# A seventh weight unit loaded ahead of the expert stage, with three rounded buffers in place of four until it is used

## The chip, the cores and the metric

The program runs on 1 core of one Trainium2 chip. The metric is device time in microseconds (us). Three runs of the kernel before gave 1814.45, 1812.17 and 1812.78 us, a median of 1812.78.

## What is computed

The reference is three layers over 256 tokens of width 1024 in float32. The first is a mixer layer (sparse attention beside a state space model) with a feed-forward part, the second a short convolution with a feed-forward part, the third a mixer of two attentions followed by a mixture of experts. The change touches the mixture of experts alone:

```python
h  = rms_norm(x, ffn_norm)
g_w, g_idx   = top_k(softmax(h @ w_group + b_group), 1)      # one of 8 groups per token
top_v, top_i = top_k(e_sel, 2)                                # two of its 8 experts
gate = g_w * softmax(top_v)
out  = sum over the two experts e of gate[e] * ((silu(h @ w1[e]) * (h @ w3[e])) @ w2[e])
x    = x + out
```

`w1` and `w3` are 1024x512 and `w2` is 512x1024, 64 experts each: 192 matrices of 2 MB, all of which are read from HBM once.

## The kernel before

**Units.** Each of the 192 expert matrices is one unit: a tile of 128 partitions by 4096 words. A group of experts has 24 units, in the order of the list `MOE` (lines 661 to 664): w1 and w3 of experts 0, 1 and 2, then w2 of expert 0, w1 and w3 of expert 3, w2 of expert 1 and so on, so that units 6, 9, 12 and 15 are w2 products. There are 8 groups, 192 units; `m_unit` counts the units that TensorE has finished.

**Stages of a unit.** SyncE loads it into one of six slots of `ring` (`expert_load`, line 794). ScalarE writes the rounded copy, here called the high copy, into one of four buffers `w_hi` (`first_hi` at line 1742 for units 0 to 3, ahead of the stage, and `split_hi` at line 1974 for the rest). VectorE subtracts it from the raw weights and leaves the low copy in the slot itself (`split_lo`, line 2566). TensorE multiplies with both: 16 matmuls in `expert_in` (line 1510) or `expert_out` (line 1541). The high copy of a unit may be written when its buffer's last unit is finished, and a slot is loaded again when its unit is finished:

```python
sp.wait_ge(m_unit, n * NM + (u - SLOTS + 1))        # line 810: load of unit u waits for unit u - 6
act.wait_ge(m_unit, n * NM + (u - HI_SLOTS + 1))    # line 1973: high copy of unit u waits for unit u - 4
```

**Order on each engine.** All of it is written out by hand, and each engine works its list in order.

- ScalarE, behind unit u: it copies the product out (`hidden_raw`, line 1987), for some u it computes the silu (line 1992), the rounded half of the hidden layer (`hidden_hi`, line 1996) or copies the turned selection (line 1982), and then it writes the high copy of unit u + 4.
- VectorE, at position u: it writes the low copy of unit u + 3, then for some u `hidden` (line 2699, the product of silu and the other half) and `hidden_lo` (line 2704), and at u = 8 the selection of the next group (line 2637). `hidden` of expert e stands behind the low copies of units 5, 7, 9 and 12 for e = 0, 1, 2 and 3, and `hidden_lo` behind those of units 6, 8, 10 and 13.
- `hidden_hi` of expert e on ScalarE waits for `hidden` of that expert on VectorE. It stands at u = 3, 5, 7 and 10 for the first four experts.
- TensorE: unit u, then at u = 2, 4, 6 and 9 the `fold` of experts 0 to 3 (line 1524, 16 small matmuls), which needs both products of that expert copied out, and `hidden` of the expert before.

**Ahead of the stage.** The six slots are filled as the last units of the layer before leave them (lines 796 to 799), and the sixth load waits for `out2_11`, the last product of the output projection. ScalarE writes high copies 0, 1 and 2 before the projection is finished. The fourth buffer of `w_hi` lies where the high half of the projection's second weight unit lies, so high copy 3 is written once `out2_11` is ready (`first_hi(3)`, line 1960). VectorE writes low copies 0 and 1. Then come the norm, the router and the gathering of the tokens of group 0, and TensorE begins unit 0. `passes` (how often all groups are gone through) is 1 with these inputs.

The kernel's functions:

Of the kernel before, what the change touches and what calls it, by code (L numbers as in the profile page):

```python
# [254 lines left out]
def program(nc, d, out):  # L255
    with ExitStack() as ctx:
# [146 lines left out]
        w_hi = [first_w_hi, second_w_hi, carve(SLOT, of=arena_r), last_hi]  # L403
# [266 lines left out]
        MOE_SLOT = [(W.next + u) % SLOTS for u in range(len(MOE))]  # L670
        MOE_BEFORE = [W.last[s] for s in MOE_SLOT[:SLOTS]]
        MOE_BASE = [W.dmas[s] * 16 for s in MOE_SLOT]
        PER_SLOT = len(MOE) // SLOTS
        NM = len(MOE)

# [46 lines left out]
        def _(sp):  # L722
# [73 lines left out]
            for u, (kind, e) in enumerate(PREFETCH):  # L796
                if MOE_BEFORE[u]:
                    sp.wait_ge(*MOE_BEFORE[u])
                expert_load(kind, e, u)
# [18 lines left out]

            with sp.Fori(0, passes) as p:
                with sp.Fori(0, N_GROUPS - 1) as g:  # L820
                    n = sp.snap(p * N_GROUPS + g)
                    rest_of_group(n, g * PER_GROUP)
                    first_of_group(n, g * PER_GROUP + PER_GROUP)
                n = sp.snap(p * N_GROUPS + (N_GROUPS - 1))
                rest_of_group(n, N_EXPERTS - PER_GROUP)
                with sp.If(p + 1 < passes):
                    first_of_group(n, 0)
            sp.wait_ge(out_ready, 2)
# [9 lines left out]
        def _(pe):  # L838
# [596 lines left out]
            def occupy(n):  # L1435

                for _ in range(n):
                    mm(bank("idle"), w_hi[0][:, 0:P], w_hi[0][:, P:P + 512], start=True, stop=True)
# [61 lines left out]
            def expert_in(u, n):  # L1500
# [6 lines left out]
                u_hi, u_lo = w_hi[u % HI_SLOTS], ring_r[MOE_SLOT[u]]  # L1507
# [20 lines left out]
            def expert_out(u, n, p=None):  # L1528
# [10 lines left out]
                u_hi, u_lo = w_hi[u % HI_SLOTS], ring_r[MOE_SLOT[u]]  # L1539
# [75 lines left out]
            occupy(3)  # L1615
            with pe.Fori(0, passes) as p:
                with pe.Fori(0, N_GROUPS - 1) as g:
                    n = pe.snap(p * N_GROUPS + g)
                    pe.wait_ge(m_xg_lo, n + 1)
                    for u, (kind, e) in enumerate(MOE):  # L1620
                        if kind == "w2":
                            expert_out(u, n)
                        else:
                            expert_in(u, n)
                        if u == 0:
                            with pe.If(g < 1):
                                pe.wait_ge(r_gate, 2)
                                gates_of(n)
                        if u in FOLD_AT:
                            fold(FOLD_AT[u], n)  # L1630
                        if u == SEND_AT:
                            with pe.If(g > 0):
                                send_back(n)
                        if u == SELT_AT:
                            turn_selection(n)
                        if u == GATHER_AT:
                            pe.wait_ge(m_selT, n + 1)
                            gather(n + 1)
                            gates_of(n + 1)
# [20 lines left out]
                with pe.If(p + 1 < passes):  # L1660
                    pe.wait_ge(m_scd, n * 4 + 6)
                    gather(n + 1)


        @block.scalar
        def _(act):
# [72 lines left out]
            def first_hi(u):  # L1739

                act.wait_ge(landed[MOE_SLOT[u]], MOE_BASE[u] + 16)
                A(w_hi[u], ring[:, MOE_SLOT[u], :], ACT.Copy).then_inc(m_hi, 1)
# [217 lines left out]
            first_hi(3)  # L1960
# [7 lines left out]
            def split_hi(u, n):  # L1968

                at = u % NM  # L1970

                act.wait_ge(landed[MOE_SLOT[at]], n * (16 * PER_SLOT) + (MOE_BASE[at] + 16 * (u // SLOTS + 1)))
                act.wait_ge(m_unit, n * NM + (u - HI_SLOTS + 1))
                A(w_hi[u % HI_SLOTS], ring[:, MOE_SLOT[at], :], ACT.Copy).then_inc(m_hi, 1)  # L1974
# [36 lines left out]

            with act.Fori(0, passes) as p:
                with act.Fori(0, N_GROUPS - 1) as g:
                    n = act.snap(p * N_GROUPS + g)
                    for u in range(NM):
                        results(u, n)
                        if u == GATHERED_AT:
                            gathered(n + 1)
                        if u < NM - 1:
                            split_hi(u + HI_SLOTS, n)  # L2020
                    act.wait_ge(m_unit, n * NM + NM)
                    for i in range(2):
                        result_hi(i)
                    split_hi(NM - 1 + HI_SLOTS, n)
# [23 lines left out]
                with act.If(p + 1 < passes):  # L2048
                    for u in range(NM, NM + HI_SLOTS):
                        split_hi(u, n)  # L2050
                    gathered(n + 1)
            n = act.snap(passes * (4 * N_GROUPS))
# [10 lines left out]
        def _(dve):  # L2063
# [498 lines left out]
            def split_lo(u, n):  # L2562

                dve.wait_ge(m_hi, n * NM + (u + 1))
                raw = ring[:, MOE_SLOT[u % NM], :]
                V.tensor_tensor(ring_r[MOE_SLOT[u % NM]][:, :], raw, w_hi[u % HI_SLOTS].bitcast(F32), ALU.subtract).then_inc(m_lo, 1)  # L2566

            split_lo(0, 0)
            split_lo(1, 0)
# [112 lines left out]
            split_lo(2, 0)  # L2682
# [28 lines left out]

            with dve.Fori(0, passes) as p:
                n = dve.snap(p * N_GROUPS)
                with dve.If(p > 0):
                    dve.wait_ge(m_sc, n * 4 + 4)
                    for i, (tc, h) in enumerate(RES):
# [278 lines left out]
```

## Time and profile before

| | |
|---|---|
| median of 3 runs | 1812.78 us (1812.17 to 1814.45) |
| the profiled execution | 1814.1 us |
| its span, first to last instruction | 1812.3 us |
| granted TensorE clock over the span | 0.994 |
| TensorE busy | 1733.4 us, 96% |
| VectorE busy | 1575.9 us, 87% |
| ScalarE busy | 1219.2 us, 67% |
| GpSimd busy | 125.3 us, 7% |
| loads of expert weights | 192 of 2048 KB |

The span is 1.8 us shorter than the profiled execution's own time, which is 1.3 us above the median. Times in a timeline are counted from the first instruction. A row of a timeline has the start and the length in us, the engine, the line of the kernel, what is written and read with its shape, how many instructions are merged in it, and in square brackets how long the engine had been idle and what ended that. A length runs to the time at which the result is written; the next instruction of the engine starts some 0.1 us before that.

### The profile page before, as it was taken

What the parts mean: (1) busy time and instruction counts of PE and PEld (TensorE: products, weight loads), DVE (VectorE), ACT (ScalarE), POOL (GpSimd) and SP (SyncE); (2) the same over time, 40 slices, a digit from 0 to 9 for tenths busy, and PEclk for the clock granted to TensorE, in tenths of its full rate; (3) what the DMA queues carried; (4) which work ended last, traced back from release to release, by engine and by line L of the source; (5) the groups of instructions that cost most, each with busy time, mean ns of one, the idle gap of its engine ahead of it and who ended that gap; (6) DMA issues with size and microseconds to landing.
All of it is one profiled execution on the core that took longest, in us unless ns stands there. A gap on an engine that the chain in (4) does not pass through costs nothing.

```text
span 1812.3 us, 25062 instructions
## 1 busy us (share of the span) xinstructions
PE 1733.4 (96%) x9708; PEld 1478.8 (82%) x9708; DVE 1575.9 (87%) x1383; ACT 1219.2 (67%) x955; POOL 125.3 (7%) x142
## 2 busy tenths in 40 slices
PE   8999999999999999989999999989999999999998
PEld 7977888889888889978877877778777777787776
DVE  6777777789577786587999999999999999999997
ACT  5555454443334355446788989889898898888886
POOL 1255000000000010441000000000000000000000
PEclk9999999999999999999999999999999999999999
DMA  7521345553354555226799999999999999999995
GB/s 288 193 93 71 140 178 202 208 239 148 121 192 177 203 200 217 96 118 244 309 427 428 428 429 428 429 429 428 429 428 428 430 427 428 428 428 429 428 426 241
DMA packets 41389, 544.25 MB, mean 300 GB/s; under 512 B 4720, under 2 KB 4848, under 8 KB 6640
## 3 DMA queue, kind: packets, MB, share of 16 engines
q1 hardware_dynamic: 41328, 543.39, 72.8%
q8 instruction: 43, 0.70, 0.2%
q14 instruction: 18, 0.15, 0.0%
HBM read 542.33 MB, written 1.05 MB: 300 GB/s over the span
## 4 chain that ended last, share of the span: by engine, by line
PE 60%; DMA 13%; issue 7%; ACT 6%; DVE 5%; POOL 0%; DVEq 0%; ACTq 0%; SPq 0%
PE psum L1510 16%; DMA ring<-in_w 13%; PE psum L1053 9%; PE psum L1070 7%; PE psum L893 6%; PE psum L1055 4%; PE psum L1524 4%; ACT arena_r L1974 4%; PE psum L1541 3%; DVE ring_r L2566 2%; PE psum L936 2%; PE psum L1273 1%; PE psum L953 1%; PE psum L1448 1%; PE psum L1416 1%
## 5 line engine op out<-in xcount | busy, mean ns | idle before, releaser
L2566 DVE TENSOR_TENSOR ring_r<-ring,arena_r 128x4096 fp32r<-128x4096 f32 x191 | 842.4, 4418 | 16.0 <-ACT arena_r L1974 12.6
L1974 ACT ACTIVATE arena_r<-ring 128x4096 fp32r<-128x4096 f32 x188 | 682.5, 3630 | 63.7 <-DMA ring<-in_w 62.8
L1510 PE MATMUL psum<-arena_r,stream_r 128*128 128x512 f32 x1024 | 409.2, 400 | 10.5 <-DVE stream_r L2656 7.9
L1510 PE MATMUL psum<-ring_r,stream_r 128*128 128x512 f32 x1024 | 401.1, 392 | 0.0
L1053 PE MATMUL psum<-stream_r,arena_r 128*128 128x512 f32 x704 | 250.6, 398 | 2.1 <-DVE stream_r L2111 1.7
L1510 PEld LDWEIGHTS psum<-arena_r,stream_r 128*128 128x128 f32 x1024 | 193.6, 189 | 55.3 <-DVE ring_r L2566 9.6
L1758 ACT ACTIVATE arena_r<-ring 128x3072 fp32r<-128x3072 f32 x40 | 111.0, 2776 | 181.2 <-DMA ring<-in_ffn 181.2
L1510 PEld LDWEIGHTS psum<-ring_r,stream_r 128*128 128x128 f32 x1024 | 193.5, 189 | 39.0 <-issue 0.5
L1055 PE MATMUL psum<-stream_r,ring_r 128*128 128x256 f32 x704 | 197.6, 281 | 0.0
L1541 PE MATMUL psum<-arena_r 128*128 128x512 f32 x512 | 162.9, 399 | 11.6 <-DVE arena_r L2704 10.6
L1053 PEld LDWEIGHTS psum<-stream_r,arena_r 128*128 128x128 f32 x704 | 132.2, 188 | 35.1 <-issue 3.1
L1541 PE MATMUL psum<-ring_r,arena_r 128*128 128x512 f32 x512 | 159.5, 392 | 0.0
L893 PE MATMUL psum<-stream_r,ring_r 128*128 128x256 f32 x776 | 142.7, 284 | 0.0
L1055 PEld LDWEIGHTS psum<-stream_r,ring_r 128*128 128x128 f32 x704 | 133.0, 189 | 1.5
L2256 DVE TENSOR_TENSOR ring_r<-ring,arena_r 128x3072 fp32r<-128x3072 f32 x40 | 134.1, 3351 | 0.0
L1541 PEld LDWEIGHTS psum<-arena_r 128*128 128x128 f32 x512 | 94.3, 189 | 37.5 <-DVE arena_r L2704 13.5
L893 PEld LDWEIGHTS psum<-stream_r,ring_r 128*128 128x128 f32 x776 | 114.9, 192 | 0.9 <-issue 0.8
L1541 PEld LDWEIGHTS psum<-ring_r,arena_r 128*128 128x128 f32 x512 | 96.7, 189 | 21.0
L1070 PE MATMUL psum<-arena_r 128*128 128x512 f32 x352 | 101.4, 391 | 0.0
L1524 PEld LDWEIGHTS psum<-small,arena 128*128 128x128 f32 x512 | 63.8, 191 | 43.3 <-ACT arena L1987 31.0
L893 PE MATMUL psum<-stream_r,arena_r 128*128 128x256 f32 x416 | 94.0, 283 | 0.3 <-DVE ring_r L2086 0.3
L1524 PE MATMUL psum<-small,arena 128*128 128x64 f32 x512 | 67.5, 275 | 26.6 <-ACT arena L1987 26.5
(354 smaller groups left out, 2438.6 us busy)
## 6 DMA issues: line engine op xcount, KB each, us to landing
ring<-in_w SPq DMA_DIRECT2D x192, 2048.0 KB, 13.0
ring<-in_ffn SPq DMA_DIRECT2D x44, 1536.0 KB, 6.3
ring<-in_w_in SPq DMA_DIRECT2D x8, 2048.0 KB, 7.9
ring<-in_out_w SPq DMA_DIRECT2D x7, 2048.0 KB, 7.9
ring<-in_in_w SPq DMA_DIRECT2D x6, 2048.0 KB, 10.9
ring<-in_l_in SPq DMA_DIRECT2D x8, 1536.0 KB, 9.1
ring<-in_proj SPq DMA_DIRECT2D x2, 2048.0 KB, 8.6
ring<-in_in_w SPq DMA_DIRECT2D x2, 1024.0 KB, 9.8
```

The lines of the kernel that those rows point to most:

```text
L893: last = mm(dst, w[:, at:at + width], a[:, k, :], start=(k == 0 and i == 0), stop=(k == KD - 1 and i == 2))
L936: last = mm(bank(name)[:, 0:width], a[:, k, tc * P:(tc + 1) * P], w[:, k * n:k * n + width], start=(k == 0 and i == 0), stop=(k == KD - 1 ...
L1053: mm(gu[b % 2][m], u_hi[:, at:at + P], both_halves[:, :, k, :], start=(k == 0), stop=(k == KD - 1), skip_group_check=True)
L1055: return mm(gu[b % 2][m][:, 1, :], u_lo[:, at:at + P], xnT_r[:, k, :], start=False, stop=(k == KD - 1), skip_group_check=True)
L1070: last = mm(bank(f"ffn{n}_{tc}{h}"), a[:, b % 2, tc * P:(tc + 1) * P], w[:, 2048 + h * 512:2560 + h * 512], start=(start and i == 0), stop ...
L1510: last = mm(dst, xg[:, k, :], b[:, k * D_EXPERT:(k + 1) * D_EXPERT], start=(k == 0 and b is u_hi), stop=(k == KD - 1 and b is u_lo))
L1524: last = mm(psum[:, T_BANK, (i * NE + j) * CAP:(i * NE + j + 1) * CAP], h_raw[:, e % 2, i, j * P:(j + 1) * P], turn, start=True, stop=True)
L1541: return mm(psum[:, Y_BANK[h], :], hT[:, e % 3, j, :], b[:, j * D + h * 512:j * D + (h + 1) * 512], start=(e == 0 and j == 0 and b is u_hi ...
L1758: A(arena_r[:, FFN_HIGH[n][nxt % FFN_RING]:][:, 0:FFN_WORDS], ring[:, slot, 0:FFN_WORDS], ACT.Copy).then_inc(w_high, 1)
L1974: A(w_hi[u % HI_SLOTS], ring[:, MOE_SLOT[at], :], ACT.Copy).then_inc(m_hi, 1)
L2256: V.tensor_tensor(ring_r[slot][:, 0:FFN_WORDS], ring[:, slot, 0:FFN_WORDS], arena_r[:, FFN_HIGH[n][nxt % FFN_RING]:][:, 0:FFN_WORDS].bitca ...
L2566: V.tensor_tensor(ring_r[MOE_SLOT[u % NM]][:, :], raw, w_hi[u % HI_SLOTS].bitcast(F32), ALU.subtract).then_inc(m_lo, 1)
```

## The change

- The seventh unit (unit 6) is loaded ahead of the stage as well. It goes into the words of the arena that held the projection's high half, which were the fourth rounded buffer, `last_hi`. The load stands right behind the sixth load in SyncE's list and waits for `out2_11`. Its low copy is left in the same place.
- With that, units 0 to 8 of the first group use three rounded buffers in turn; from unit 9 on there are four again. `first_hi(3)` ahead of the stage is gone. ScalarE writes high copy u + 3 behind unit u for u = 0 to 6, behind unit 6 also high copy 10, and high copy u + 4 from there on.
- In the first group, loads 7 to 12 wait for units 0 to 5, the slot that they go into; from load 13 on, load u waits for unit u - 6 as before. The slots of all later units are one further round the ring.
- The first group of the first pass is written out ahead of the loops on every engine, and the loop over groups starts at 1. For a second pass, the first group is written out again inside the `If` at the end of the pass.

```diff
-        w_hi = [first_w_hi, second_w_hi, carve(SLOT, of=arena_r), last_hi]
+        w_hi = [carve(SLOT, of=arena_r), last_hi, first_w_hi, second_w_hi]
+        seventh, seventh_lo = arena[:, D:D + SLOT], last_hi
...
+        AHEAD = SLOTS + 1
...
+        def high_of(u, early):
+            if early and u < 3 * 3:
+                return w_hi[(2, 3, 0)[u % 3]]
+            return w_hi[u % HI_SLOTS]
...
@@ SyncE
-            for u, (kind, e) in enumerate(PREFETCH):
+            for u in range(SLOTS):
                 if MOE_BEFORE[u]:
                     sp.wait_ge(*MOE_BEFORE[u])
-                expert_load(kind, e, u)
+                first_load(u)
+            sp.wait_ge(*O.ready("out2_11"))
+            first_load(SLOTS)
             sp.wait_ge(x_rows, NT)
...
+            for u in range(AHEAD, NM):
+                sp.wait_ge(m_unit, u - AHEAD + 1 if u <= AHEAD + SLOTS - 1 else u - SLOTS + 1)
+                first_load(u)
+            first_of_group(0, PER_GROUP)
             with sp.Fori(0, passes) as p:
-                with sp.Fori(0, N_GROUPS - 1) as g:
+                with sp.Fori(1, N_GROUPS - 1) as g:
...
@@ TensorE
+            group_of_units(0, True, True)
             with pe.Fori(0, passes) as p:
-                with pe.Fori(0, N_GROUPS - 1) as g:
+                with pe.Fori(1, N_GROUPS - 1) as g:
...
                 with pe.If(p + 1 < passes):
                     pe.wait_ge(m_scd, n * 4 + 6)
                     gather(n + 1)
+                    n = pe.snap(n + 1)
+                    group_of_units(n, True)
...
@@ ScalarE
             square_row(5, 1)
-            first_hi(3)
...
+            def split_hi(u, n, early=False):
+                at_work = HI_SLOTS - 1 if early and u <= 3 * 3 else HI_SLOTS
+                act.wait_ge(*unit_landed(u, n, early))
+                act.wait_ge(m_unit, n * NM + (u - at_work + 1))
+                A(high_of(u, early), raw_of(u, early), ACT.Copy).then_inc(m_hi, 1)
...
+            def group_of_units(n, early=False):
+                for u in range(NM):
+                    results(u, n)
+                    if u == GATHERED_AT:
+                        gathered(n + 1)
+                    if early and u <= SLOTS:
+                        split_hi(u + 3, n, True)
+                    if u < NM - 1 and not (early and u < SLOTS):
+                        split_hi(u + HI_SLOTS, n, early)
...
+            group_of_units(0, True)
...
@@ VectorE
+            def group_of_units(n, following, opening, early=False):
+                if opening:
+                    gates_in_fold(n)
+                for u in range(NM):
+                    split_lo(u + 3, n, early and u + 3 < NM)
+                    if u in FOLD_AT:
+                        hidden(FOLD_AT[u], n)
+                    if u in TURN_AT:
+                        hidden_lo(TURN_AT[u], n)
...
+            group_of_units(0, 1, True, True)
```

## Rows read from the trace of the kernel before

**Rows 1.** The page: busy time, share of the span and instructions of each engine.
```profile
PE 1733.4 (96%) x9708; PEld 1478.8 (82%) x9708; DVE 1575.9 (87%) x1383; ACT 1219.2 (67%) x955; POOL 125.3 (7%) x142
```

**Rows 2.** Stretches: length, busy time per engine, TensorE clock, DMA share, GB/s.
```profile
866.00:878.00 12.00, 10.94 (x65) 9.12 (x64) 9.49 (x30) 3.56 (x4) 0.00 (x0) 1.00 0.14 39
880.00:960.00 80.00, 75.91 (x383) 62.47 (x382) 79.65 (x32) 69.85 (x45) 0.00 (x0) 1.00 1.00 424
...
1000.00:1790.00 790.00, 748.14 (x3772) 620.15 (x3770) 776.76 (x336) 695.28 (x418) 0.00 (x0) 1.00 1.01 428
```

**Rows 3.** Loads of units 6, 13, 16 and 29: issue, and time to landing.
```profile
L794 SPq DMA_DIRECT2D ring<-in_w x1: 342/342/342, 876.1 to 876.1; - x1
...
DMA to landing us min/median/max: 8.5/8.5/8.5
...
L794 SPq DMA_DIRECT2D ring<-in_w x1: 333/333/333, 908.0 to 908.0; - x1
...
DMA to landing us min/median/max: 11.4/11.4/11.4
...
L794 SPq DMA_DIRECT2D ring<-in_w x1: 333/333/333, 921.7 to 921.7; - x1
...
DMA to landing us min/median/max: 13.1/13.1/13.1
...
L794 SPq DMA_DIRECT2D ring<-in_w x1: 333/333/333, 988.5 to 988.5; - x1
...
DMA to landing us min/median/max: 10.0/10.0/10.0
```

**Rows 4.** Timeline of ScalarE behind units 0, 2, 3 and 5.
```profile
876.42 3.63 ACT L1974 ACTIVATE arena_r<-ring 128x4096 fp32r<-128x4096 f32 x1
...
886.25 3.63 ACT L1974 ACTIVATE arena_r<-ring 128x4096 fp32r<-128x4096 f32 x1
...
892.69 0.42 ACT L1996 ACTIVATE arena_r<-arena 128x256 fp32r<-128x256 f32 x1 [2.33 <-DVE arena L2699]
...
893.28 3.63 ACT L1974 ACTIVATE arena_r<-ring 128x4096 fp32r<-128x4096 f32 x1
...
902.35 3.62 ACT L1974 ACTIVATE arena_r<-ring 128x4096 fp32r<-128x4096 f32 x1
```

**Rows 5.** Timeline of VectorE: low copies 3 to 8 and one hidden step.
```profile
879.23 13.09 DVE L2566 TENSOR_TENSOR ring_r<-ring,arena_r 128x4096 fp32r<-128x4096 f32 x3
892.24 0.42 DVE L2699 TENSOR_TENSOR arena<-psum,arena 128x256 f32<-128x256 f32 x1
892.57 4.42 DVE L2566 TENSOR_TENSOR ring_r<-ring,arena_r 128x4096 fp32r<-128x4096 f32 x1
...
897.24 4.42 DVE L2566 TENSOR_TENSOR ring_r<-ring,arena_r 128x4096 fp32r<-128x4096 f32 x1
...
901.91 4.41 DVE L2566 TENSOR_TENSOR ring_r<-ring,arena_r 128x4096 fp32r<-128x4096 f32 x1
```

**Rows 6.** Chain that ended last, TensorE: a fold, units 7 and 8, fold 3.
```profile
883.64 1.73 PE psum L1524 x16
...
904.11 7.35 PE psum L1510 x32
```
```profile
915.83 1.10 PE L1524 MATMUL psum<-small,arena 128*128 128x64 f32 x8 [0.73 <-ACT arena L1987]
```

**Rows 7.** VectorE's low copies 957 to 984; unit 23; a stretch behind it.
```profile
L2566 DVE TENSOR_TENSOR ring_r<-ring,arena_r 128x4096 fp32r<-128x4096 f32 x7 | 31.0, 4424 | 1.6 <-ACT arena_r L1974 1.3
```
```profile
982.94 0.50 PE L1541 MATMUL psum<-arena_r 128*128 128x512 f32 x1 [1.79 <-DVE arena_r L2704]
```
```profile
980.00:985.00 5.00, 3.21 (x12) 2.27 (x11) 5.00 (x3) 4.22 (x3) 0.00 (x0) 0.87 1.02 436
```

**Rows 8.** The page: DMA queue of instructions. Timeline of ScalarE at the end.
```profile
q8 instruction: 43, 0.70, 0.2%
```
```profile
1803.55 0.60 ACT L2055 ACTIVATE xn<-psum 128x512 f32<-128x512 f32 x1 [0.41 <-PE psum L1604]
```

## Prediction before the result

> **What bounds the kernel now.** I began with the page. TensorE is busy for 96% of the span [rows 1], which suggests a kernel bound by TensorE, but that share is a mean over stages. So I cut the span into stretches. From 880 us on, the DMA engines are busy for the whole of every stretch at 424 to 428 GB/s [rows 2]: the expert stage is a stream of weights. A unit of 2048 KB takes 2.097 MB / 428 GB/s = 4.9 us. The stage ends when the last unit has landed and has been worked. Anything that moves the landings moves the end by as much, and nothing else does.
>
> The stretch ahead of it is the opening that the change aims at: between 866 and 878 us the DMA engines have a share of 0.14 [rows 2]. Six units have landed, and the load of unit 6 waits for unit 0 and is issued at 876.1 [rows 3]. One more load in that hole would put every later landing 4.9 us earlier, if the queue never runs dry afterwards.
>
> The same table shows why that "if" matters. From 880 to 960 us VectorE is busy for 79.65 of 80 us, against 776.76 of 790 (98.3%) later [rows 2]. So two things are saturated at once in the first 80 us. Whoever makes VectorE late there makes TensorE late, then the loads that wait for TensorE, then perhaps the stream.
>
> How much lateness does the stream bear? A load issued into an empty queue lands 8.5 us later. Load 13 lands 11.4 us after its issue, load 16 after 13.1, load 29 after 10.0 [rows 3]. What is above 8.5 is time that the load spent queued behind others, and so its reserve: 2.9 us for load 13, 4.6 for load 16, 1.5 for load 29.
>
> **The DMA side of the change.** Loads 6 to 12 land 4.9 us earlier, load 7 being issued at 876.1, where load 6 was, and so on. Load 13, however, still waits for unit 7, the same unit as before, while the queue ahead of it is 4.9 us shorter. Its reserve of 2.9 becomes -2.0. So even with no delay in the computation the gain is at most 2.9 us, not 4.9, and each further microsecond by which unit 7 is late costs one. The seventh load itself costs nothing: it waits for the same product as the sixth, so nothing on SyncE's list is held up, and the row of norm weights behind it is wanted only at the end. The DMA engines are idle then [rows 2]; without that hole it would cost its 4.9 us.
>
> **The compute side.** High copy 3 is no longer written ahead, and ScalarE is one unit less ahead of VectorE until unit 9. I follow VectorE copy by copy. Before, low copies 3, 4 and 5 run back to back from 879.23, 13.09 us for three, hence 4.34 apart [rows 5].
>
> 1. High copy 3 takes the place that high copy 4 had behind unit 0: 876.42 plus 3.63 is 880.05 [rows 4]. Low copy 3 starts at 880.1 instead of 879.2: **0.9 us late**.
> 2. High copy 5 takes the place of high copy 6: 886.25 plus 3.63 is 889.9 [rows 4]. Low copy 5 starts there instead of at 879.23 + 2 x 4.34 = 887.9: **2.0 late**.
> 3. Here is the step that costs. Behind low copy 5 VectorE does `hidden` (892.24) [rows 5], ScalarE waits for it (2.33 us idle), rounds it at 892.69, and starts the next high copy at 893.28 [rows 4]. That is 5.4 us after low copy 5 started. Before, the copy in that place was number 7, needed two low copies later, so its 3.63 us were hidden. Now it is number 6, the very next that VectorE wants. So VectorE waits for ScalarE, which has just waited for VectorE: 889.9 + 5.4 + 3.63 = 898.9 instead of 892.57 [rows 5], **6.4 late**.
> 4. Low copy 7 follows at once, high copy 7 being finished by then (898.9 + some 0.7 + 3.6 = 903.2, against 898.9 + 4.7 = 903.6): still 6.4 late.
> 5. The same loop again through `hidden` of expert 1. Before, 902.35 - 897.24 = 5.1 us from low copy 7 to the high copy [rows 4, 5]; now 903.6 + 5.1 + 3.6 = 912.4 instead of 901.91: **10.5 late**.
> 6. Behind unit 6 ScalarE writes two high copies and has its old lead back. VectorE, which had only 0.35 us idle in 80 [rows 2], keeps the 10.5.
>
> **From there to the stream.** Unit 7 has the fold of expert 2 in front, and that fold needs `hidden` of expert 1, which stands behind low copy 7: 903.6 + 4.3 + 0.4 = 908.4. Add 1.75 for the fold, 3.9 for the unit (half of 7.35 and the end of the last matmul) [rows 6] and 0.2 to the issue: load 13 is issued at 914.3 and lands 8.5 later, at 922.8. Before, it landed at 908.0 + 11.4 = 919.4. Load 12, one unit's 4.9 us ahead of that and now 4.9 us earlier, has landed at 909.6, so the engines run dry for several us, which the old kernel never does here.
>
> Load 16 waits for unit 10, and unit 10 stands behind fold 3, which waits for ScalarE [rows 6] and by way of the high copy before that for `hidden` of expert 2, behind low copy 9. So its issue is 10.5 late: 921.7 + 10.5 + 8.5 = 940.7. Before, it landed at 921.7 + 13.1 = 934.8. The stream is now **5.9 us behind** the old one. The landings between (14 and 15) come no later by this count.
>
> Afterwards VectorE catches up in its idle time, but a landing lost is not won back. One more place is tight: load 29, reserve 1.5 [rows 3], waits for unit 23, and unit 23 for `hidden_lo` behind low copy 24 [rows 7]. VectorE's idle time up to there is 0.35 to 960 [rows 2] and 1.6 after it [rows 7], so it is still 10.5 - 1.9 = 8.6 late against a stream that is 5.9 late: another 8.6 - 5.9 - 1.5 = 1.2. TensorE's granted clock is 0.87 in the stretch around that unit, so part of it at 1.2 GHz and the rest at 2.4 GHz, after an idle time of 1.79 us [rows 7]. I assume the same fall again in the same place; without it unit 23 ends 1.6 us sooner and the 1.2 is gone.
>
> **Sum.** 5.9 + 1.2 = 7.1 us. The tail behind the last landing is not touched. The rest of the edit goes at nothing: a branch per group is removed, and the straight first group is the same instructions in the same order. Against the profiled execution that is 1814.1 + 7.1 = 1821.2; the difference carried to the median is 1812.78 + 7.1 = **1819.9 us**.
>
> Bounds of what the trace does not show. Issue to landing into an empty queue is 8.5 us in the one row that has it [rows 3] and cannot be above the 10.0 of load 29, which had others ahead of it; it could be 0.2 less or more elsewhere, and I take 8.5. Entering the loop at group 1 instead of 0 costs between 0 and the 0.3 us by which the engines' issue times scatter. Idle times of TensorE of 3 to 4 us, new in this stage, may lower its clock in units 6 and 8; priced by the fall in unit 23 that is up to 1.6 us each, but both stand in front of VectorE's wait and not behind it, so I take 0 and keep 1.6 for the range.
>
> On the landing time the rows and a rule part. The Trainium skill, DMA: Bandwidth & Descriptors (Anatomy of one DMA), gives about 2.0 us plus the bytes over 436 GB/s, which for a unit is an estimate of 6.8 us; by it every landing of the starved queue would come 1.7 us sooner and the sum would be 5.4. It is written for the path through GpSimd, and the row of this kernel's own load says 8.5.
>
> **The rivals.**
> - *The waits are absorbed (not slower).* Place: unit 7, on which load 13 waits. If VectorE's loss stayed at the 2.0 us of step 2, load 13 would land at 908.0 + 2.0 + 8.5 = 918.5, 0.9 us earlier than before: 1811.9. With no loss at all 2.9 are won: 1809.9. It decides the case if unit 7 is less than 2.9 us late. For it: the exchange of step 3 is argued from order, not seen. Against it: the 2.33 us in which ScalarE waits for `hidden` [rows 4] show the loop half closed already. Chance 0.10.
> - *Only one loop bites.* If high copy 8 were ready by some reserve I missed, VectorE stays 6.4 late and load 16 lands at 921.7 + 6.4 + 8.5 = 936.6, 1.8 us late: 1814.6. Chance 0.10.
> - *Instruction fetch.* The `If` at the end of the pass now holds a whole group, which one pass jumps over. Fetches of instructions take 0.2% of 16 engines' 1812 us for 43 packets, 1.35 us each [rows 8]; ScalarE stands 0.41 us idle there [rows 8], so 0.9 us would come through: 1820.8, and 1821.7 with as much at the loop's entry. Chance 0.10. The Trainium skill, Runtime: NRT & Kernel Launch (Instruction fetch mechanics), has it that a taken branch to a page outside the two held ones stalls for a fetch; no row shows such a stall.
> - *The clock falls on the path.* 1.6 us more: 1821.5. Chance 0.10.
> - *The seventh unit does not come early.* Its load could only be late by standing behind the sixth. Even then, from load 13 on the time is set by the units, so the sum is the same.
>
> **How the numbers follow.** The forecast has 0.60, with 1817.8 to 1820.8 as its own range. 0.2% of the time is 3.6 us, about what a measurement of this kernel can tell from no change. The first two rivals lie within it, and I leave 0.03 for a gain of more: the reserve of load 13 forbids it. Same 0.17. Slower 0.80. The range goes from 1814.3, just under the second rival, to 1822.8, the clock and the fetch together; it leaves out the first rival and a little above.
>
> **What would show it.** Right: ScalarE's first high copy behind unit 0 is number 3; two idle times of VectorE of 4 to 4.5 us at about 894.5 and 908.3, ended by ScalarE's high copy; low copy 8 at 912.4; a hole in the DMA row around 909 to 918 and load 13 issued at 914; the seventh unit landed by 872. Wrong: a DMA share of 1.00 through 905 to 925, or low copy 8 before 905.

## The result, and the profile after

| | before | after |
|---|---|---|
| median | 1812.68 us of 4 runs | 1823.59 us of 4 runs (1822.76 to 1824.36) |
| the profiled execution | 1814.1 | 1824.4 |
| its span | 1812.3 | 1822.5 |

The ratio is 1.0060, with a 95% interval of 1.0045 to 1.0075: 10.9 us slower. The direction is as forecast, and the time is 3.7 us above the forecast and 0.8 us above the range.

The page of the kernel after, and the three stretches of [rows 2] in it, the first two 0.86 us earlier because unit 0 begins that much earlier here (columns as in [rows 2]):

```profile
PE 1737.9 (95%) x9708; PEld 1480.8 (81%) x9708; DVE 1574.8 (86%) x1383; ACT 1200.6 (66%) x942; POOL 125.0 (7%) x142
...
q8 instruction: 49, 0.80, 0.2%
```
```profile
865.14:877.14 12.00, 11.03 (x66) 9.17 (x65) 9.49 (x30) 2.28 (x3) 0.00 (x0) 1.00 0.49 187
879.14:959.14 80.00, 71.11 (x341) 57.88 (x340) 70.60 (x28) 65.70 (x41) 0.00 (x0) 0.96 0.88 360
1000.00:1790.00 790.00, 750.15 (x3767) 622.30 (x3766) 775.27 (x338) 678.43 (x407) 0.00 (x0) 0.99 1.01 428
```

The change does what it says: the hole in the transfers ahead of the stage is partly filled, a share of 0.49 in place of 0.14 [rows 2]. But in the 80 us behind it VectorE is busy for 70.60 us instead of 79.65, and the DMA engines, which were never idle there, have a share of 0.88. At 360 GB/s in place of 424 [rows 2] they move 5.1 MB less, which is 2.4 units or 12 us of the stream. Less the 4.9 us of the unit that was loaded early, some 7 us are lost there by this estimate. From 1000 us on the stream runs at its old rate again.

Where VectorE and ScalarE lost it, in their timelines (copies 3 and 4, 5, `hidden`, copies 6, 7 and 8 on VectorE; then high copy 3, `hidden_hi` of expert 0, high copy 6, `hidden_hi` of expert 1 and high copy 8 on ScalarE):

```profile
879.21 8.76 DVE L2621 TENSOR_TENSOR ring_r<-ring,arena_r 128x4096 fp32r<-128x4096 f32 x2 [0.67 <-ACT arena_r L2021]
889.04 4.42 DVE L2621 TENSOR_TENSOR ring_r<-ring,arena_r 128x4096 fp32r<-128x4096 f32 x1 [1.07 <-ACT arena_r L2021]
893.38 0.42 DVE L2754 TENSOR_TENSOR arena<-psum,arena 128x256 f32<-128x256 f32 x1
898.06 4.42 DVE L2621 TENSOR_TENSOR arena_r<-arena,arena_r 128x4096 fp32r<-128x4096 f32 x1 [4.26 <-ACT arena_r L2021]
...
902.74 4.42 DVE L2621 TENSOR_TENSOR ring_r<-ring,arena_r 128x4096 fp32r<-128x4096 f32 x1
...
911.49 4.43 DVE L2621 TENSOR_TENSOR ring_r<-ring,arena_r 128x4096 fp32r<-128x4096 f32 x1 [3.99 <-ACT arena_r L2021]
```
```profile
875.56 3.62 ACT L2021 ACTIVATE arena_r<-ring 128x4096 fp32r<-128x4096 f32 x1
...
893.84 0.42 ACT L2043 ACTIVATE arena_r<-arena 128x256 fp32r<-128x256 f32 x1 [4.35 <-DVE arena L2754]
894.42 3.61 ACT L2021 ACTIVATE arena_r<-arena 128x4096 fp32r<-128x4096 f32 x1
...
907.53 0.42 ACT L2043 ACTIVATE arena_r<-arena 128x256 fp32r<-128x256 f32 x1 [4.74 <-DVE arena L2754]
907.85 3.61 ACT L2021 ACTIVATE arena_r<-ring 128x4096 fp32r<-128x4096 f32 x1
```

The two engines wait for each other in turn. `hidden` ends at 893.80, ScalarE has waited 4.35 us for it, then writes high copy 6, and VectorE has waited 4.26 us for that. The same again behind copy 7, with 4.74 and 3.99. Low copy 8 starts at 911.49, where it started at 901.91 [rows 5]: 9.6 us late, and 10.4 if counted from unit 0.

The loads that answer to [rows 3] (units 13, 14, 15, 16, 27 and the last one, 191), and after them the loads of 27 and 191 in the kernel before:

```profile
L830 SPq DMA_DIRECT2D ring<-in_w x1: 328/328/328, 913.4 to 913.4; - x1
...
DMA to landing us min/median/max: 7.4/7.4/7.4
...
L830 SPq DMA_DIRECT2D ring<-in_w x1: 327/327/327, 921.5 to 921.5; - x1
...
DMA to landing us min/median/max: 7.3/7.3/7.3
...
L830 SPq DMA_DIRECT2D ring<-in_w x1: 328/328/328, 925.1 to 925.1; - x1
...
DMA to landing us min/median/max: 9.7/9.7/9.7
...
L830 SPq DMA_DIRECT2D ring<-in_w x1: 327/327/327, 931.2 to 931.2; - x1
...
DMA to landing us min/median/max: 8.6/8.6/8.6
...
L825 SPq DMA_DIRECT2D ring<-in_w x1: 327/327/327, 985.9 to 985.9; - x1
...
DMA to landing us min/median/max: 9.5/9.5/9.5
...
L825 SPq DMA_DIRECT2D ring<-in_w x1: 327/327/327, 1784.3 to 1784.3; - x1
...
DMA to landing us min/median/max: 17.0/17.0/17.0
```
```profile
L794 SPq DMA_DIRECT2D ring<-in_w x1: 332/332/332, 977.6 to 977.6; - x1
...
DMA to landing us min/median/max: 11.2/11.2/11.2
...
L794 SPq DMA_DIRECT2D ring<-in_w x1: 328/328/328, 1775.8 to 1775.8; - x1
...
DMA to landing us min/median/max: 15.8/15.8/15.8
```

Landings are issue plus landing time. Load 13 lands at 920.8 against 919.4, load 14 at 928.8 against 925.0 and load 15 at 934.8 against 929.9; load 16 at 939.8 against 934.8, 5.0 late (5.8 counted from unit 0); load 27 at 995.4 against 988.8, 6.6 late; load 191 at 1801.3 against 1791.6, 9.7 late. So 3.1 us were lost behind unit 27, and not by loads that were issued too late: they were lost at loads 30 and 191, which were issued 11.6 and 17.0 us ahead of their landings. The first place is in ScalarE's timeline, high copies 29 and 30:

```profile
1005.21 3.64 ACT L2021 ACTIVATE arena_r<-ring 128x4096 fp32r<-128x4096 f32 x1 [0.73 <-DMA ring<-in_w]
...
1011.64 3.64 ACT L2021 ACTIVATE arena_r<-ring 128x4096 fp32r<-128x4096 f32 x1 [0.58 <-DMA ring<-in_w]
```

Both copies start as their unit lands, 6.43 us apart where the stream brings one in 4.9, although load 30 was issued 11.6 us ahead. A smaller part is behind the last unit, on SyncE: the first two of the three output stores, after, and then the second one before.

```profile
1817.29 0.34 SPq L873 DMA_DIRECT2D out<-x  x1
1817.95 1.26 SPq L875 DMA_DIRECT2D out<-x  x1
```
```profile
1808.54 0.34 SPq L831 DMA_DIRECT2D out<-x  x1
```

The middle store takes 0.9 us more to issue. Writing out the first group and giving it another order are thus two suspects, and the runs take them apart.

### The profile page after: what moved, and what is told of

The parts are those of the page before. It is cut to its first block, busy times and chain, and to the rows that moved or that the text cites. A ratio compares the mean times of both kernels' runs of the same rounds, so it can differ in the third digit from the quotient of the medians.

```text
span 1822.5 us, 24836 instructions
## 1 busy us (share of the span) xinstructions
PE 1737.9 (95%) x9708; PEld 1480.8 (81%) x9708; DVE 1574.8 (86%) x1383; ACT 1200.6 (66%) x942; POOL 125.0 (7%) x142
## 4 chain that ended last, share of the span: by engine, by line
PE 51%; DVE 11%; issue 11%; DMA 11%; ACT 6%; POOL 0%; DVEq 0%; ACTq 0%; SPq 0%
DMA ring<-in_w 10%; PE psum L1554 10%; PE psum L1097 8%; DVE ring_r L2621 7%; PE psum L1114 6%; PE psum L937 6%; PE psum L1099 4%; ACT arena_r L2021 4%; PE psum L1568 3%; PE psum L1585 2%; PE psum L980 2%; PE psum L1317 1%; PE psum L997 1%; PE psum L1492 1%; PE psum L1460 1%
## 5 line engine op out<-in xcount | busy, mean ns | idle before, releaser
L1585 PE MATMUL psum<-arena_r 128*128 128x512 f32 x520 | 163.7, 397 | 13.1 <-DVE arena_r L2759 10.4
## 6 DMA issues: line engine op xcount, KB each, us to landing
ring<-in_in_w SPq DMA_DIRECT2D x6, 2048.0 KB, 10.4
```

The lines of the kernel that those rows point to most:

```text
L1585: return mm(psum[:, Y_BANK[h], :], hT[:, e % 3, j, :], b[:, j * D + h * 512:j * D + (h + 1) * 512], start=(e == 0 and j == 0 and b is u_hi ...
```

## The experiments

Ratios are to the kernel before on the same chip, with the 95% interval; medians are of 10 or 11 runs unless another count stands. "Over before" is the median less that of the kernel before in the same series (1813.19, 1813.54, 1813.09 and 1813.12 us in the four series), 10.9 us for the changed kernel. In the first expectations theory A is that of the prediction (order, then stream), and theory B that the written-out group costs something by itself; the later expectations each say what theory A is there.

**Writing the group out and nothing else.** The buffers, order and loads of before, but group 0 ahead of the loops on every engine:

```diff
-        w_hi = [carve(SLOT, of=arena_r), last_hi, first_w_hi, second_w_hi]
+        w_hi = [first_w_hi, second_w_hi, carve(SLOT, of=arena_r), last_hi]
...
-            sp.wait_ge(*O.ready("out2_11"))
-            first_load(SLOTS)
...
+            first_hi(3)
...
-                    if early and u <= SLOTS:
-                        split_hi(u + 3, n, True)
```

> The first group written out ahead of the loops and nothing else: six units loaded ahead, four rounded buffers, high copy 3 written ahead, as in the kernel before. Theory A (the loss comes from VectorE and ScalarE waiting for each other, and what comes after load 16 follows from the queue of loads having run short): no difference, 1812.7 within 1.5 us, every landing within 1 us of before. Theory B (writing the group out costs by itself, through more fetches of instructions on the DMA engines and a long jump at the end): 3 to 5 us slower, the landings slipping where instructions are fetched.

1815.77 us, ratio 1.0013 (1.0004 to 1.0022), 2.6 us over before. So this part of the edit is not free, though 2.6 us is less than the 3 to 5 of theory B.

**The seventh load not early.** The changed kernel, with unit 6 loaded behind unit 0 as before:

```diff
-            sp.wait_ge(*O.ready("out2_11"))
-            first_load(SLOTS)
...
+            sp.wait_ge(m_unit, 1)
+            first_load(SLOTS)
             for u in range(AHEAD, NM):
```

> As the changed kernel, but the load of unit 6 waits for unit 0 instead of the last product of the projection, so nothing is loaded in the hole. Theory A: from load 13 on each load is issued when its unit is finished and the queue is dry, so the 4.9 us lead was already lost there: load 13 still lands at about 920.8, the total within 1.5 us of the changed kernel's 1823.6. Rival (the early load is worth something that the rest hides): 4.9 us slower than the changed kernel, 1828.5.

1822.52 us of 4 runs, ratio 1.0050 (1.0035 to 1.0065), 9.3 us over before; with the load early 1.0060 (1.0045 to 1.0075) and 10.9. The intervals overlap, and load 13 lands at 920.0 here: the load that the change is about wins nothing that shows, and nearly the whole loss stands without it.

**The order on VectorE.** `hidden` of experts 0 and 1 moves ahead of the low copy at its place, so that ScalarE need not wait for that copy:

```diff
                 for u in range(NM):
+                    sooner = early and u in (2, 4)
+                    if sooner:
+                        hidden(FOLD_AT[u], n)
                     split_lo(u + 3, n, early and u + 3 < NM)
-                    if u in FOLD_AT:
+                    if u in FOLD_AT and not sooner:
                         hidden(FOLD_AT[u], n)
```

> As the changed kernel, but in the first group VectorE does the hidden step of experts 0 and 1 ahead of low copies 5 and 7 instead of behind them, so that ScalarE does not wait for it before high copies 6 and 8. Theory A: both waits of VectorE of 3.8 to 4.5 us go, low copy 8 starts 2 to 3 us later than before instead of 10.5, load 13 lands about 2 us earlier than in the kernel before, and the total is 1810 to 1813. Theory B: the same less 3 to 5 us that remain, 1814 to 1817. Rival (the third buffer itself is what is short, not the order): VectorE still waits for high copies 6 and 8, total 1820 or more.

1815.70 us, ratio 1.0011 (1.0002 to 1.0020), 2.5 us over before: two operations of 0.42 us that change places with a low copy take 8.4 of the 10.9 us back. Its VectorE timeline, low copies 5 and 6, and the stretch:

```profile
890.36 4.43 DVE L2621 TENSOR_TENSOR ring_r<-ring,arena_r 128x4096 fp32r<-128x4096 f32 x1 [0.73 <-ACT arena_r L2021]
894.93 4.43 DVE L2621 TENSOR_TENSOR arena_r<-arena,arena_r 128x4096 fp32r<-128x4096 f32 x1
```
```profile
880.00:960.00 80.00, 75.13 (x373) 61.48 (x371) 78.30 (x31) 72.35 (x45) 0.00 (x0) 1.00 0.96 400
```

The idle time of 4.26 us is gone, VectorE is busy for 78.30 us of 80, and the DMA share is 0.96. This is the loop of the prediction's step 3, opened at one end. The total is where theory B had it (1814 to 1817).

**The order on ScalarE.** The other end: high copies 6 and 8 ahead of the `hidden_hi` that waits.

```diff
+                    swapped = early and u in (3, 5)
+                    if swapped:
+                        hidden_raw(u, n)
+                        split_hi(u + 3, n, True)
+                        hidden_hi(TURN_AT[u], n)
...
```

> As the changed kernel, but ScalarE writes high copies 6 and 8 ahead of the rounded halves of hidden 0 and 1, which is the other way to break the same loop. Theory A: low copy 8 about 2.5 us later than in the kernel before, load 13 lands about 0.7 us earlier than there, total 1811 to 1814. If the order did not matter: 1823.

1819.38 us of 6 runs, ratio 1.0029 (1.0017 to 1.0041), 6.2 us over before: 4.7 us are back, a miss against what was expected. VectorE still waits for high copies 7 and 8:

```profile
901.66 4.42 DVE L2629 TENSOR_TENSOR ring_r<-ring,arena_r 128x4096 fp32r<-128x4096 f32 x1 [1.79 <-ACT arena_r L2021]
...
906.85 4.43 DVE L2629 TENSOR_TENSOR ring_r<-ring,arena_r 128x4096 fp32r<-128x4096 f32 x1 [0.43 <-ACT arena_r L2021]
```

Low copy 8 starts at 906.85, between the 911.49 of the changed kernel and the 901.91 of before [rows 5]. What runs ahead on ScalarE here is a copy of 3.63 us, and what it passes is later by as much; on VectorE it was an operation of 0.42 us. That this is why the form wins less is read from these rows alone, and no run tests it.

**What in the written-out group costs.** First, without the group inside the `If` at the end of the pass (a second pass is left out; so it is in the other kernels below that have a short or no `If` or a loop from 1 or 2 on one engine alone, and with one pass the work timed is complete), on SyncE, TensorE, ScalarE and VectorE:

```diff
                 with sp.If(p + 1 < passes):
                     first_of_group(n, 0)
-                    rest_of_group(n + 1, 0)
-                    first_of_group(n + 1, PER_GROUP)
...
-                    n = pe.snap(n + 1)
-                    group_of_units(n, True)
```

> As e1, but the first group of a second pass, which is never executed with these inputs, is left out of the If at the end of the pass, so that the jump at the end is as short as in the kernel before; a second pass would be computed wrongly. Theory A (the jump makes SyncE fetch instructions between its last stores): the gap from the second to the third output store goes back from 1.8 us to some 0.4 us, and the total falls by about 1 us against e1, to 1814.5. Rival (the stall belongs to the place of the code, not to the jump): no change, 1815.5.

1815.53 us, ratio 1.0011 (1.0002 to 1.0020), 2.0 us over before. The middle store is issued in 0.34 us again; with the long `If` in the same kernel it took 1.75:

```profile
1810.20 0.34 SPq L857 DMA_DIRECT2D out<-x  x1
```
```profile
1806.92 1.75 SPq L859 DMA_DIRECT2D out<-x  x1
```

The cause of the stall at the stores is thus shown: it comes and goes with what the `If` holds. In the changed kernel a packet of the instruction queue, q8, travels during that store, and with the short `If` none does. But 2 us remain. Next, group 1 written out too (loops from 2), to double them if they are per group:

```diff
             group_of_units(0, True, True)
+            group_of_units(1, False)
...
-                with pe.Fori(1, N_GROUPS - 1) as g:
+                with pe.Fori(2, N_GROUPS - 1) as g:
```

> As e5, with the second group written out ahead of the loops too, which doubles what the first one adds: TensorE fetches another group's code, five to six pages, while the stream runs. Theory A (each fetched page can hold one DMA engine up, and a hitch of up to 1.5 us in the landings stays): one or two hitches more than e5 in the stretch from 1110 to 1230 us, total 0 to 3 us above e5, most likely 1.5. Rival (the cost of writing the group out has nothing to do with fetches): equal to e5 within 0.5 us, no new hitches.

1815.97 us, ratio 1.0012 (1.0003 to 1.0021), 2.4 us over before. That is 0.4 us more than with one group, where theory A had most likely 1.5 and its rival less than 0.5. The intervals are too wide to tell twice the cost from the same. The rows side with theory A: in the profiled execution loads 30, 72 and 190 land 6.1, 6.2 and 5.7 us behind the one before, each with a packet of instructions in that gap, and from the landing of load 17 to that of load 191 it takes 855.8 us, against 853.3 with one group and 851.9 before. Its total is low all the same (1815.2), because load 17 had landed 3.0 us earlier than in the run with one group.

**Combinations.** By the diffs above: the VectorE order with the load not early, then the VectorE order with the short `If`.

> As e3 (hidden first), but the load of unit 6 waits for unit 0. Now the computation is only 2.8 us late, so the lead of the early load should not be wholly lost. Theory A: by the reserve of load 13 in the kernel before (2.9 us), the stream without the early load is just not starved by 2.8 us, the landings stay as in e1, total 1814 to 1817, that is within 2 us of e3; the early load is worth at most 2.9 us. Rival (the early load is worth its full 4.9 us once the order is mended): 1820 or more.

1814.84 us, ratio 1.0010 (1.0001 to 1.0020), 1.3 us over before; with the early load it was 2.5. Even with the order mended the early load shows no gain.

> As e3 (hidden first) without the first group of a second pass in the If. Theory A: about 1 us less than e3, 1814.7, still not under the kernel before, because the fetches of the group's code remain. If it comes under 1812 the seventh unit does pay once its order and the jump are mended.

1814.59 us, ratio 1.0006 (0.9997 to 1.0015), 1.1 us over before. This is the best form of the change. It is still not under the kernel before, from which it can't be told apart.

**On which engine.** The first is the short form with TensorE's loop as it was; the second is the kernel before with TensorE's first group alone written out. The diff is that of the first, the second turns it round:

```diff
-            group_of_units(0, True, True)
             with pe.Fori(0, passes) as p:
-                with pe.Fori(1, N_GROUPS - 1) as g:
+                with pe.Fori(0, N_GROUPS - 1) as g:
```

> As e5 (first group written out, no second pass), but TensorE's own list keeps the loop of the kernel before, so that it does not fetch the group's code a second time. If TensorE's fetches cause the 2 us that writing the group out costs: 1813.5 within 1 us, 43 packets in the queue of instructions as before, and no hitch of over 1 us in the landings between 990 and 1240 us. If it is the other engines' lists: 1815.5 as e5.

> The kernel before with TensorE's first group alone written out ahead of its loop. If TensorE's fetches are the cause: 1815.5 as e5, one hitch of 1.0 to 1.5 us near a fetch between 990 and 1110 us. If not: 1813.5 as the kernel before.

1812.53 us, ratio 1.0000 (0.9991 to 1.0009), and 1814.67 us, ratio 1.0010 (1.0001 to 1.0019): 0.6 us under before and 1.6 over. The two intervals just overlap, so the rows have to bear it out that the cost is TensorE's. The DMA view of both for 1092 to 1101 us (packets, MB, share of 16 engines), and ScalarE's high copies there, all but the one at 1095.08 started by their landing; first TensorE alone:

```profile
q8 instruction: 1, 0.02, 0.8%
```
```profile
1094.22 3.63 ACT L1977 ACTIVATE arena_r<-ring 128x4096 fp32r<-128x4096 f32 x1 [0.86 <-DMA ring<-in_w]
...
1100.67 3.63 ACT L1977 ACTIVATE arena_r<-ring 128x4096 fp32r<-128x4096 f32 x1 [2.34 <-DMA ring<-in_w]
```

Then all but TensorE:

```profile
q1 hardware_dynamic: 265, 3.85, 100.5%
```
```profile
1095.08 3.62 ACT L1999 ACTIVATE arena_r<-ring 128x4096 fp32r<-128x4096 f32 x1
...
1099.82 3.64 ACT L1999 ACTIVATE arena_r<-ring 128x4096 fp32r<-128x4096 f32 x1 [0.64 <-DMA ring<-in_w]
```

A packet of instructions travels in the full stream, and the copy behind its landing starts 6.45 us after the one before it instead of 4.74. Over the whole run the instruction queue q8 moves 43 packets before and with TensorE's loop kept, 47 with TensorE's group written out (with or without the others), 49 with the group in the `If` as well, and 52 with two groups. Between 990 and 1700 us, in the middle of the stream, it moves none before and with TensorE's loop kept, and 5 with the group written out on TensorE, by the same view:

```profile
q8 instruction: 5, 0.08, 0.0%
```

With all but TensorE written out, another queue (q14) moves three packets of half that size in this stretch, and no landing there is late.

The meeting of packet and late landing can be counted. The 14 profiled executions of this case have 2436 landings from load 18 on, 4.9 us apart as a rule. Of these, 34 come more than 5.2 us behind the one before. Five of them are load 27, whose issue is late in those runs. Of the other 29, 26 have a q8 packet in the gap, while of all 2436 gaps only 177 have one. So where a landing was late without a late issue, a fetch was nearly always there. The reverse does not hold: 122 of the 148 packets delayed no landing by that much.

**One load made later.** In the short form of the written-out group, load 27 waits for one unit more:

```diff
-            first_of_group(0, PER_GROUP)
+            for u, (kind, e) in enumerate(PREFETCH):
+                sp.wait_ge(m_unit, NM - SLOTS + u + 1 + (1 if u == 3 else 0))
+                expert_load(kind, PER_GROUP + e, u)
```

> As e5, but load 27 alone waits for one unit more, so it is issued some 3.7 us later, about 7.5 us ahead of the time at which it used to land (11.2 less 3.7). Theory R1 (a load lands on time if issued 8.5 us ahead, as the prediction took it): it lands some 1 us late, and all behind it too; total 1 us over e5. Theory R2 (a full stream needs some 10 us): it lands 2 to 2.5 us late. No effect on landings before it.

1815.34 us, ratio 1.0012 (1.0003 to 1.0022). That is 2.3 us over before, against 2.0 without the later load. The total doesn't tell the two apart. The rows do. Load 27 in the short form, then with the later issue:

```profile
L811 SPq DMA_DIRECT2D ring<-in_w x1: 328/328/328, 977.7 to 977.7; - x1
...
DMA to landing us min/median/max: 11.2/11.2/11.2
```
```profile
L811 SPq DMA_DIRECT2D ring<-in_w x1: 328/328/328, 980.1 to 980.1; - x1
...
DMA to landing us min/median/max: 9.4/9.4/9.4
```

This execution runs 1.2 us ahead of the other at unit 26, so the load is issued 3.6 us later and lands 1.9 later. It had 1.7 us to give, not the 11.2 - 8.5 = 2.7 of the prediction's rule. But that does not make 9.4 us a floor for every load in the full stream: in the changed kernel load 19 lands 9.1 us after its issue and no later behind load 18 than the stream brings one in (4.90), and in the run with the VectorE order and the load not early load 27 does so with 9.2.

**The changed kernel with the short `If`.**

> The changed kernel with the first group of a second pass left out of the If, as e5 is to e1. If the parts add up: the gap between the last output stores goes, 0.9 us less than the changed kernel's 1823.6, so 1822.7; two waits of VectorE of 3.8 to 4.5 us at about 894 and 907 as in the changed kernel, and load 13 issued when the queue is empty. If the long jump cost more than the one gap: 1821 or less.

1821.96 us of 5 runs, ratio 1.0049 (1.0035 to 1.0063), 8.8 us over before against 10.9. VectorE's two idle times are there as expected, 4.26 us ahead of 898.05 and 3.99 us ahead of 911.47, and the middle store takes 0.34 us. The stall at the stores is 0.9 of the 2.1; the rest is within the intervals.

## Why the prediction was right or wrong

**Right: the compute side.** All six steps happened. High copy 3 is the first behind unit 0; VectorE's idle times are 4.26 and 3.99 us; low copy 8 at 911.5 was forecast for 912.4, with all of the difference in the 0.86 us by which unit 0 began sooner (875.56 against 876.42 [rows 4]). The run with `hidden` ahead shows it as the cause, and its price in the end: 10.9 - 2.5 = 8.4 us.

**Right in the main: the DMA side.** The seventh unit had landed at 869.5. Load 13 was issued at 913.4 (914.3 less the 0.86 is 913.4), and the transfers ran dry ahead of it, as in this stretch (columns as in [rows 2]):

```profile
909.00:914.00 5.00, 4.34 (x22) 3.32 (x21) 2.51 (x1) 5.00 (x3) 0.00 (x0) 1.00 0.00 0
```

Load 16 landed 5.8 us late counted from unit 0, where 5.9 was the sum. The rival by which the seventh unit does not come early gave the same sum, and the run without it is not above the changed kernel. The rivals "the waits are absorbed" and "only one loop bites" are refuted by the second idle time of 3.99 us.

**Luck in how near the 5.9 came.** The step had load 16 set the loss by its own late issue. But load 15 was already 5.8 us late counted from unit 0, and load 16 landed 4.95 us behind it, as the stream brings them in. The loss arose at loads 13, 14 and 15, and two of its terms were off, in opposite directions.

- Landing into an empty queue: loads 13 and 14 landed 7.4 and 7.3 us after their issue, not 8.5 [rows 3]. The Trainium skill, DMA: Bandwidth & Descriptors (Anatomy of one DMA), whose rule for the path through GpSimd gives an estimate of 6.8, was nearer to these two than the row was. Load 16 took 8.6, with load 15 still ahead of it.
- TensorE's clock: the bounds priced a fall in units 6 and 8 at nothing, since both stand in front of VectorE's wait. Unit 8 does not. It starts at 915.97, when low copy 8 is written, after 2.63 us in which TensorE was idle, and more than half of it runs at 1.2 GHz:

```profile
915.97 0.79 PE L1554 MATMUL psum<-arena_r,stream_r 128*128 128x512 f32 x1 [2.63 <-DVE ring_r L2621]
```
```profile
916.00:920.00 4.00, 4.00 (x11) 3.20 (x12) 4.00 (x2) 3.22 (x2) 0.00 (x0) 0.58 0.96 410
```

It ends at 921.32, after 5.35 us in place of 3.7 (half of the 7.35 of [rows 6]), and load 14, which waits for it, was issued at 921.5. Up to 1.6 us of load 14's lateness is thus the clock's. The rival "the clock falls on the path" had that event right, but it did not come on top of the sum. How much of it reached load 16 no run shows.

**Wrong: the size of a load's reserve in the running stream, and the place of the last loss.** The step said that all above 8.5 is reserve, that load 29 is tight and that the clock falls again at unit 23. The clock did not fall there: load 29 is only as late as the stream. It fell earlier, in unit 8 as above and in the stretch below, ahead of which TensorE had been idle for 1.82 us. There its mean was 0.72, so part of the time at 1.2 GHz and the rest at 2.4:

```profile
894.00:900.00 6.00, 6.00 (x28) 5.21 (x29) 1.94 (x1) 6.00 (x6) 0.00 (x0) 0.72 1.01 429
```

This one lies in front of VectorE's wait, as the bounds had it, and low copy 8 came no later than forecast. Load 27 was the tight one instead. It was issued 8.3 us late and landed 6.6 late, so it had 1.7 us to give, as in the run with the later load, and not 2.7. The stream ahead of it was 5.8 late, so it lost 0.8 us. Counted from unit 0 the landings are 5.8 us late at load 16 and 7.5 at load 27 (6.6 + 0.9), where the sum had 7.1. That these are near is partly luck too: of the 1.7 between them load 27 explains 0.8, and 0.7 were lost at load 20, where a packet of instructions lies (next point).

**Wrong, and the reason for the miss: "The rest of the edit goes at nothing: a branch per group is removed, and the straight first group is the same instructions in the same order."** The instructions are the same, but q8 moves more of them: 49 packets in place of 43 [rows 8]. The bound of 0 to 0.3 us covered the entry of the loop alone. The runs price it in two parts. TensorE's written-out group costs 1.6 us alone and 2.0 with the other engines' in the short form, by medians whose intervals reach some 1.6 us to either side. The group in the `If` costs 0.9 us at SyncE's second store, and 1.4 in the kernel whose only edit is the group written out. The instruction-fetch rival, with a chance of 0.10, had the right resource. It had the wrong engine: ScalarE's idle time at the jump is 0.39 us after and was 0.41 [rows 8]. And it missed the larger part, since it asked what the fetching engine waits for and not what a fetch does to the stream. The Trainium skill, Runtime: NRT & Kernel Launch (Instruction fetch mechanics), has a taken branch to a page that is not held stall for a fetch. SyncE's row of 1.26 us against 0.34 agrees with that.

Added up against the profiled executions: -0.9 for the earlier unit 0, 7.5 up to load 27, 2.8 from there to the end of the last unit (which is 9.4 late) and 0.8 at the stores make 10.2, and so do the spans. The 2.8 and the 0.8 are in no term of the prediction's sum.

**Open.** Why one fetched packet delays a landing by some 1.5 us was not tried. Its own time is 0.8% of 16 engines' 9 us, 1.2 us on one of them. One reading is that a unit has landed only when the slowest of its parts has, and that a packet counts only where it meets that part; that would fit the 122 packets of 148 that delayed nothing much. It is an argument and not shown. That fetches cause the late landings at all rests on the kernels with and without TensorE's written-out group and on the count of packets in late gaps; no run fetched without changing the code. Of the 3.1 us between loads 27 and 191, load 30 took 1.5 and load 191 took 1.5, and both have a packet in their gap (1008.4 in 1005.2 to 1011.6, and 1798.0 in 1794.8 to 1801.2). In the kernel before, the packet near the last load starts at 1795.8, 4.2 us after that load has landed. Which packets meet a landing thus shifts with the timing of the kernel. Not tried either is the seventh unit in its best order with TensorE's first group left in its loop.

## What to carry to other kernels

A buffer fewer is a change of order: where two engines hand work to and fro, write down which copy the other engine needs next, because a lead of one unit on either side can be what keeps a wait on each from closing into a loop. A prefetch is worth only what its queue keeps, so ask at once which later load is issued at the old time, and take its reserve from a run in which it is issued later, not from a landing into an empty queue. And a loop unrolled for one group isn't free in a kernel bound by its transfers: leave the engine with the most instructions in its loop, as the run that kept TensorE's loop did, with the time of before (ratio 1.0000).

## What was not expected of the hardware

- Instructions that TensorE's written-out group adds travel with the weights: four packets more on the instruction queue (43 to 47), 1.6 to 2.0 us by the medians, lasting to the end of the kernel. Of 29 landings that were late without a late issue, 26 have such a packet in the gap; most packets delay nothing.
- An `If` that is not taken can cost by what stands in it: an output store just behind it took 1.26 and 1.75 us to issue with a group's 24 loads in its body, and 0.34 without.
- A load of 2048 KB landed 7.2 to 8.6 us after its issue into an empty or nearly empty queue in these two kernels. In the full stream one came 9.1 us after its issue without being late, and another 9.5 after and 0.8 us late.
